# Modulation rows of a two-layer diffusion block: the eight row blocks of a weight tile in four column groups of TensorE

## The reference, cut to what matters

```python
# d = D_MODEL = 1024; w_mod: (DEPTH, d, 6 * d); b_mod: (DEPTH, 6 * d)
        mod_l = jax.nn.silu(c) @ w_mod[layer] + b_mod[layer]
        mod_c = jax.nn.silu(c_ctx) @ w_mod[layer] + b_mod[layer]
        sh1, sc1, g1, sh2, sc2, g2 = jnp.split(mod_l[:, None, :], 6, axis=-1)
        csh1, csc1, cg1, csh2, csc2, cg2 = jnp.split(mod_c, 6)
```

## Time and profile before

| | us |
|---|---|
| median of 3 runs | 3995.61 |
| lowest, highest | 3993.08, 3996.35 |
| the profiled execution's own time | 3988.36 |
| its span in the profile | 3986.6 |
| TensorE busy | 3170.7 (80%) |
| VectorE busy | 1925.9 (48%) |
| ScalarE, GpSimd busy | 739.1, 1444.5 |
| mean granted TensorE clock | 0.894 |

### The profile page before, as it was taken

How to read it: one execution, slowest core, us unless ns; L and a number is a source line. 1 busy time by engine, 2 the same in 40 slices (tenths; PEclk the granted TensorE clock), 3 DMA queues, 4 the chain that set the end, 5 groups by cost and what they waited for, 6 DMA issues and landing times. The chain is left out here.

```text
span 3986.6 us, 27787 instructions
## 1 busy us (share of the span) xinstructions
PE 3170.7 (80%) x8516; PEld 1539.3 (39%) x8516; DVE 1925.9 (48%) x4693; ACT 739.1 (19%) x1716; POOL 1444.5 (36%) x1540
## 2 busy tenths in 40 slices
PE   6978975688788888878749676688887597897888
PEld 2433433233333333333334234344333264543663
DVE  1014626766666667676440365766776314213100
ACT  0011321221212222221100311222212011122100
POOL 0000001777777777777600001777777200000000
PEclk8989787889999999989979698899898898998999
DMA  5114122999999999999932144999999642433333
GB/s 184 64 54 170 45 86 105 395 419 419 419 413 418 416 415 414 416 415 408 390 132 79 50 154 153 417 419 413 417 419 414 240 138 100 128 106 121 110 128 116
DMA packets 349203, 1028.16 MB, mean 258 GB/s; under 512 B 53620, under 2 KB 58228, under 8 KB 346996
## 3 DMA queue, kind: packets, MB, share of 16 engines
q0 software_dynamic: 221184, 805.40, 50.0%
q1 hardware_dynamic: 125808, 217.57, 15.8%
q10 hardware_dynamic: 2068, 3.47, 0.3%
HBM read 1025.19 MB, written 1.15 MB: 257 GB/s over the span
## 5 line engine op out<-in xcount | busy, mean ns | idle before, releaser
L1288 PE MATMUL l_peer_experts_acc<-l_peer_experts_ring,l_peer_experts_diag 128*128 128x512 f32 x3072 | 1490.9, 636 | 359.6 <-ACT l_peer_experts_diag L1328 293.3
L1221 POOL DMA_INDIRECT weight_slots<-in_peer_u,l_peer_experts_picks x768 | 722.2, 940 | 1394.6 <-DVE l_peer_experts_picks L1415 1144.3
L1463 DVE SCALAR_TENSOR_TENSOR weight_slots<-weight_slots,l_peer_experts_h 128x1024 f32<-128x1024 f32 x768 | 937.1, 1220 | 593.5 <-DMA weight_slots<-in_peer_u,l_peer_experts_picks 587.5
L1288 PEld LDWEIGHTS l_peer_experts_acc<-l_peer_experts_ring,l_peer_experts_diag 128*128 128x128 f32 x3072 | 606.0, 204 | 1195.0 <-issue 1001.9
L1226 POOL DMA_INDIRECT l_peer_experts_ring<-in_peer_v,l_peer_experts_picks x768 | 722.1, 940 | 295.9 <-issue 199.3
L1328 ACT ACTIVATE l_peer_experts_diag<-const_ident,l_peer_experts_wgt 128x128 f32<-128x128 f32 x768 | 229.5, 387 | 172.4 <-DVE l_peer_experts_wgt L1431 172.4
L1251 PE MATMUL l_peer_experts_queries<-h_t,l_query_weights 128*128 128x512 f32 (+3 forms) x576 | 180.5, 457 | 4.1 <-PEq L61 4.1
L1310 ACT ACTIVATE l_peer_experts_h<-h_tiles 128x1024 f32<-128x1024 f32 x48 | 49.3, 1027 | 614.7 <-DVE weight_slots L1463 614.7
L1251 PEld LDWEIGHTS l_peer_experts_queries<-h_t,l_query_weights 128*128 128x128 f32 x576 | 104.7, 197 | 76.2 <-issue 67.5
L1307 ACT ACTIVATE l_peer_experts_soft<-l_peer_experts_best,l_peer_experts_low 128x16 f32<-128x16 f32 x48 | 14.7, 307 | 580.8 <-DVE l_peer_experts_low L1394 580.8
L190 PE MATMUL b_mlp_acc<-weight_slots,b_up 128*128 128x512 f32 x256 | 111.6, 599 | 12.1 <-DVEq L282 12.1
(11 more groups left out here) (423 smaller groups left out, 3311.1 us busy)
## 6 DMA issues: line engine op xcount, KB each, us to landing
weight_slots<-in_w_mod SPq DMA_DIRECT2D x24, 2048.0 KB, 8.1
weight_slots<-in_w_in SPq DMA_DIRECT2D x20, 2048.0 KB, 7.9
l_query_weights<-query_weights SPq DMA_DIRECT2D x16, 1024.0 KB, 7.8
weight_slots<-in_w_mlp_up SPq DMA_DIRECT2D x8, 2048.0 KB, 8.0
weight_slots<-in_w_mlp_down SPq DMA_DIRECT2D x8, 2048.0 KB, 7.8
weight_slots<-in_peer_u,l_peer_experts_picks POOLq DMA_INDIRECT x768, 9.0
l_peer_experts_ring<-in_peer_v,l_peer_experts_picks POOLq DMA_INDIRECT x768, 9.0
weight_slots<-in_gla_w_in SPq DMA_DIRECT2D x6, 2048.0 KB, 9.0
```

The costliest lines, as they stand in the source:

```text
L1221: pool.indirect_dma_start(u_ring[:, k % RING, :], None, u, bass.IndirectOffsetOnAxis(ap=picks[:, b % 4, k:k + 1], axis=0)).then_inc(landed ...
L1288: ins = nc.tensor.matmul(acc[:, c * BANK:(c + 1) * BANK], diag[:, k, :], v_ring[:, k % RING, c * BANK:(c + 1) * BANK], start=(k == 0), sto ...
L1463: nc.vector.scalar_tensor_tensor(row, row, 1.0, hp[:, :], ALU.mult, ALU.mult, accum_out=dots[:, b % 2, k:k + 1]).then_inc(dotted, 1)
```

## The change

The eight products of a tile no longer go to the same two rows of the bank. `silu_c` becomes 128 x 8 x 32 with zeros behind the first two columns, and each product writes 32 rows of the bank by its own quarter of TensorE's columns: the n-th goes to column group n % 4 and takes row block 2 (n % 4) + n // 4, so each group adds up two row blocks. The bank then holds four partial sums of 32 rows each, of which two rows count. VectorE copies the bank to a buffer `mod_parts` (`vector_parts`), one more product with a constant 128 x 2 of zeros and ones, `add_up`, adds the four up into the bank's rows 0 and 1 (`tensor_sums`), and VectorE adds the bias from there (`vector`). `mod_bias` is gone: the bias is loaded into the row buffer itself, in which VectorE adds, so a bias load now waits for the store that reads the buffer. SyncE loads the next weights when the products are through (`multiplied`), not when the sum is.

```diff
@@ class Modulation
+    GROUPS = 4
+    PER = KC // GROUPS
...
-        self.bias_sb = st.sb("mod_bias", [2, 2, BANK])
         self.rows = st.sb("mod_rows", [2, 2, BANK])
-        self.used, self.taken = st.sem("mod_used"), st.sem("mod_taken")
+        self.parts = st.sb("mod_parts", [P, BANK])
+        self.multiplied, self.parted, self.used, self.taken = (st.sem(f"mod_{n}") for n in ("multiplied", "parted", "used", "taken"))
...
     def tensor(self, pe, u, units):
         for step in self.share(u, units):
-            i, k = divmod(step, KC)
+            i, n = divmod(step, KC)
             slot = (self.weights.n + i) % 2
-            if k == 0:
+            j, k = n % self.GROUPS, n % self.GROUPS * self.PER + n // self.GROUPS
+            if n == 0:
                 pe.wait_ge(self.weights.loaded[slot], self.weights.count(i, i // 2))
                 if i >= len(self.banks):
                     pe.wait_ge(self.taken, i - len(self.banks) + 1)
-            ins = self.nc.tensor.matmul(self.banks[i % len(self.banks)][0:2, :], self.silu_c[:, k, :], self.weights.slots[:, slot, k, :],
-                                        start=(k == 0), stop=(k == KC - 1))
-            if k == KC - 1:
-                ins.then_inc(self.used, 1)
+            ins = self.nc.tensor.matmul(self.bank(i)[32 * j:32 * j + 32, :], self.silu_c[:, k, :], self.weights.slots[:, slot, k, :],
+                                        start=(n < self.GROUPS), stop=(n >= KC - self.GROUPS), tile_position=(0, 32 * j))
+            if n == KC - 1:
+                ins.then_inc(self.multiplied, 1)
+
+    def tensor_sums(self, pe, u, units):
+        for step in self.share(u, units):
+            i, n = divmod(step, KC)
+            if n == KC - 1:
+                pe.wait_ge(self.parted, i + 1)
+                self.nc.tensor.matmul(self.bank(i)[0:2, :], self.add_up, self.parts[:, :], start=True, stop=True).then_inc(self.used, 1)
+
+    def vector_parts(self, dve, u, units):
+        for step in self.share(u, units):
+            i, n = divmod(step, KC)
+            if n == KC - 1:
+                dve.wait_ge(self.multiplied, i + 1)
+                if i:
+                    dve.wait_ge(self.used, i)
+                self.nc.vector.tensor_copy(self.parts[:, :], self.bank(i)).then_inc(self.parted, 1)
 
     def vector(self, dve, u, units):
...
             dve.wait_ge(self.used, i + 1)
             dve.wait_ge(self.bias_loaded[s], 16 * turn + 16)
-            if turn:
-                dve.wait_ge(self.stored[s], 16 * turn)
-            ins = self.nc.vector.tensor_tensor(self.rows[:, s, :], self.banks[i % len(self.banks)][0:2, :], self.bias_sb[:, s, :], ALU.add)
+            ins = self.nc.vector.tensor_tensor(self.rows[:, s, :], self.bank(i)[0:2, :], self.rows[:, s, :], ALU.add)
...
     def sync(self, sp):
         def bias(i):
             at = self.first + i * BANK
             if i < self.tiles:
-                sp.dma_start(self.bias_sb[:, i % 2, :], self.bias[at:at + BANK].partition_broadcast(2)).then_inc(self.bias_loaded[i % 2], 16)
+                if i >= 2:
+                    sp.wait_ge(self.stored[i % 2], 16 * (i // 2))
+                sp.dma_start(self.rows[:, i % 2, :], self.bias[at:at + BANK].partition_broadcast(2)).then_inc(self.bias_loaded[i % 2], 16)
...
         for i in range(self.tiles):
-            sp.wait_ge(self.used, i + 1)
+            sp.wait_ge(self.multiplied, i + 1)
             self.weights.load(sp, i + 2)
...
             sp.dma_start(self.mod_rows[:, at:at + BANK], self.rows[:, i % 2, :]).then_inc(self.stored[i % 2], 16)
-            bias(i + 2)
+            if i:
+                bias(i + 1)
@@ stage_conditions: nc.vector.memset(silu_c[:, :, :], 0.0), then
-                nc.scalar.activation(silu_c[:, :, :], cols[:, :, :], ACT.Silu)
+                act.wait_ge(cleared, 1)
+                nc.scalar.activation(silu_c[:, :, 0:2], cols[:, :, :], ACT.Silu)
@@ stage_first_modulation, TensorE
-                mod.tensor(pe, 0, 1)
+                for i in range(mod.tiles):
+                    mod.tensor(pe, i, mod.tiles)
+                    if i == 1:
+                        pe.wait_ge(add_up_loaded, 16)
+                    if i:
+                        mod.tensor_sums(pe, i - 1, mod.tiles)
+                mod.tensor_sums(pe, mod.tiles - 1, mod.tiles)
@@ stage_first_modulation, VectorE
-                mod.vector(dve, 0, 1)
+                for i in range(mod.tiles):
+                    mod.vector_parts(dve, i, mod.tiles)
+                    mod.vector(dve, i, mod.tiles)
@@ stage_mlstm, TensorE (the same line in stage_attention)
                     last.then_inc(out_done, 1)
+                    mod.tensor_sums(pe, u, len(units))
@@ stage_mlstm, VectorE
                     last.then_inc(w_ready, 1)
-                    mod.vector(dve, u, len(units))
+                    mod.vector_parts(dve, u, len(units))
...
                     dve.sem_inc(out_taken, 1)
+                    mod.vector(dve, u, len(units))
@@ stage_gla, TensorE
                     if u + 1 < n_units:
                         keys_values(u + 1)
+                    mod.tensor_sums(pe, u, n_units)
@@ stage_gla, VectorE
                     if u:
                         take_results(u - 1)
+                        mod.vector(dve, u - 1, n_units)
                     take_scores(u)
-                    mod.vector(dve, u, n_units)
+                    mod.vector_parts(dve, u, n_units)
                 take_results(n_units - 1)
+                mod.vector(dve, n_units - 1, n_units)
@@ constants
+    add_up = np.zeros((P, 2), np.float32)
+    for c in range(2):
+        add_up[c::32, c] = 1
```

More of the change, by code:

```diff
@@ L391, in __init__ @@
         assert planned == name, (planned, name)
-        self.nc, self.weights, self.silu_c, self.banks = nc, weights, silu_c, banks
+        self.nc, self.weights, self.banks = nc, weights, banks
+        self.silu_c, self.add_up = silu_c
         self.tiles = n // BANK
         self.bias, self.mod_rows, self.first = bias, mod_rows, first
-        self.bias_sb = st.sb("mod_bias", [2, 2, BANK])
         self.rows = st.sb("mod_rows", [2, 2, BANK])
-        self.used, self.taken = st.sem("mod_used"), st.sem("mod_taken")
+        self.parts = st.sb("mod_parts", [P, BANK])
+        self.multiplied, self.parted, self.used, self.taken = (st.sem(f"mod_{n}") for n in ("multiplied", "parted", "used", "taken"))
         self.bias_loaded = [st.sem(f"mod_bias_loaded{s}") for s in range(2)]
@@ L404, in share, with bank @@
         return range(u * self.tiles * KC // units, (u + 1) * self.tiles * KC // units)
+    def bank(self, i):
+        return self.banks[i % len(self.banks)]
     def tensor(self, pe, u, units):
         for step in self.share(u, units):
-            i, k = divmod(step, KC)
+            i, n = divmod(step, KC)
             slot = (self.weights.n + i) % 2
-            if k == 0:
+            j, k = n % self.GROUPS, n % self.GROUPS * self.PER + n // self.GROUPS
+            if n == 0:
                 pe.wait_ge(self.weights.loaded[slot], self.weights.count(i, i // 2))
@@ L414, in tensor @@
                     pe.wait_ge(self.taken, i - len(self.banks) + 1)
[L415 to L418 removed]
+            ins = self.nc.tensor.matmul(self.bank(i)[32 * j:32 * j + 32, :], self.silu_c[:, k, :], self.weights.slots[:, slot, k, :],
[16 more added lines that the diff above has]
+                self.nc.vector.tensor_copy(self.parts[:, :], self.bank(i)).then_inc(self.parted, 1)
     def vector(self, dve, u, units):
         for step in self.share(u, units):
[L422 to L423 removed]
+            i, n = divmod(step, KC)
+            if n != KC - 1:
                 continue
@@ L468, in stage_conditions, with _ @@
         cols = st.sb("cols", [P, KC, 2])
-        loaded = st.sem("loaded")
+        loaded, cleared = st.sem("loaded"), st.sem("cleared")
         with nc.Block() as block:
+            @block.vector
+            def _(dve):
+                nc.vector.memset(silu_c[:, :, :], 0.0).then_inc(cleared, 1)
             @block.sync
@@ L492, in _ @@
             def _(sp):
-                for dst, src in pairs:
-                    sp.dma_start(dst, src).then_inc(loaded, 16)
+                for i, (dst, src) in enumerate(pairs):
+                    sp.dma_start(dst, src).then_inc(loaded if i else add_up_loaded, 16)
                 mod.sync(sp)
-                sp.wait_ge(loaded, 16 * len(pairs))
+                sp.wait_ge(loaded, 16 * (len(pairs) - 1))
             @block.tensor
             def _(pe):
-                mod.tensor(pe, 0, 1)
+                for i in range(mod.tiles):
[5 more added lines that the diff above has]
+                mod.tensor_sums(pe, mod.tiles - 1, mod.tiles)
             @block.vector
             def _(dve):
-                mod.vector(dve, 0, 1)
+                for i in range(mod.tiles):
+                    mod.vector_parts(dve, i, mod.tiles)
+                    mod.vector(dve, i, mod.tiles)
     mod.done()
```

(19 more changed lines are left out.)

4 lines of the change are left out of this document (1 added, 3 removed).

## The result

The changed kernel takes 4044.15 us (median of 4 runs, 4040.54 to 4046.03) against 3995.98 for the kernel before: ratio 1.0119, 95% interval 1.0103 to 1.0135. It is 48 us slower; the forecast was 4002.6, its own range 3993 to 4010, and the range with the rivals went up to 4042.

The account below looks back on a forecast made before the run. Bounds read by stage: TensorE in `gla`, VectorE and ScalarE in odd `mlstm` units, row products in even ones. Terms -2.0 + 0.5 + 3.8 + 0.6 = +2.9, clock +4, gave +7 us: 4002.6 us, range 3993 to 4010.

Parts of the forecast that it names:

- Rival C: In all changed stages: column groups do not overlap, tile time stays 7.07 us, kernel 4040.6 us; chance 0.20.
- M: Time from a tile's first row product until VectorE may read it: 7.07 us before, forecast 4.07 us.
- rival B: In all changed stages: four column groups run together, tile time 1.92 us, kernel 3978.2 us; chance 0.33.
- the order rule: On TensorE: products start in program order, so paired records overlap only partly, 9 steps in place of 16, 4.07 us.
- gla: Stage `gla`: longer looped units, +7.0 us, offset by the last two at -3.4 us; together +0.6 us.
- The loop through the one bank: In `gla`: TensorE waits until VectorE takes the previous tile's row, making units 13.35 us against 12.4.
- mlstm: Stage `mlstm`: units sum to -0.7 us, but the last store comes later; +0.5 us, bounds -3 to +4.
- The late store at the end: End of `mlstm`: store issued 4.1 us later, at 390.5 against 386.4, landing at 393.9 against 393.4.
- the clock's term: TensorE at half clock after waits in five `gla` units: between 0 and 8.5 us, half taken, +4 us.
- rival D: Overlap by pairs, but half clock after every wait in `gla` and `mlstm`: +22 on 2.9, 4020.6 us; chance 0.07.
- mod0: Stage `mod0`: last load issued near 44 and not 46.56, landing near 52; -2.0 us.
- attn: Stage `attn`: one product per unit leaves nothing to overlap, and four sums come on top; +3.8 us.

Follow-up runs that it names:

- a_shift32: The changed kernel plus an unused 32-byte-per-partition SBUF buffer ahead of its constants, so gathered buffers start at multiples of 64 again: 3992.17 us, ratio 0.9997.
- a_order: `a_shift32` with both products of each column group issued as neighbours: 4255.94 us where the kernel before took 4257.09.
- a_mlstm_thrice: `a_shift32` with the eight products of each `mlstm` tile issued three times over: ratio to the kernel before 1.0005 (0.9976 to 1.0034).
- b_slots32_only_4: A repeat on the kernel before with `weight_slots` alone starting 32 past a multiple of 64, on a slow-gather chip; the five such repeats had ratios 0.9997 to 1.0020.

## Why the prediction was wrong

- **The step that failed: that the change acts in four stages only.** The first paragraph took "some 340 us of 3986.6 us" as all that could move (the four stretches that I had read add up to 370), and gave the new constant and the moved `silu_c` a zero ("Clearing `silu_c` and the small constant lie beside the first loads: 0"). I asked when the constant is loaded, not where it lies. Its 32 bytes moved the gathered buffers, and the expert stages lost 46.6 of the 52.2 us of span; in `a_shift32` these stages are back at 1335.2 and 684.9 us. Rival C's 4040.6 us is near the result by accident: its mechanism, no overlap, did not happen.
- **M, mis-sized.** Forecast 4.07 us, measured 1.92 at full clock: the lower bound, rival B. The step that failed here is the order rule, applied to the records of a product: `a_order` (1.94 to 1.95 us) shows that the groups do not wait for each other. So the rule that the prediction cites for it from the Trainium skill ("The mechanism": matmuls start and end strictly in program order) does not hold for the records of these f32 products. The span model in the same page, "TensorE: Matmul & The Clock Gate", section "Measured speedup vs the span model", agrees with the trace: four tiles cost about one (16 records in 1.92 us; four records in one group would take 4 x 0.43 = 1.72, an estimate from the pace in the earlier trace rows).
- **gla.** The loop through the one bank was right in each link: unit = 9.28 + M, here 12.9. But the tiles of the loop took 3.3 to 3.6 us, at half clock behind their waits; that this is near the forecast's 4.07 is luck. Rival B had given -17.4 with M = 1.92, the forecast +0.6; it was -9.6.
- **mlstm.** Forecast +0.5, measured +11.6. The late store at the end was right (398.26, and 10.4 us behind the last load, so that the load no longer ends the stage). What failed is the clock's term: half of 8.5 us, put on `gla`. Faster products opened waits of 3.15 to 3.30 us in `mlstm` ahead of the products that VectorE waits for, and the eight groups of output products became 1.2 to 2.2 us longer, 12.5 together, the greater part of it on the path: with the clock kept up in `a_mlstm_thrice` the stage is still 3.7 us longer than before. The prediction had the 4.7 us wait of an odd unit in its rival B, and gave it no price; its rival D did price a fall in all eight units, at 1.7 us each, with a chance of 0.07.
- **mod0.** Forecast -2.0, measured -2.8; with this stage's code as before the same point was reached 0.7 us earlier to 1.2 us later in the table, so the size is not sharper than that.
- **attn.** Forecast +3.8, measured +5.8, and this tells nothing: with the code of before, this stretch took 153.9 to 181.8 us in the table, by the clock it was given (in `a_shift32`, 187.2 us, the window 396 to 580 has 0.68).
- **The sum outside the expert stages** was +5.6 against a forecast of +7, by errors that cancel: -9.6 and +11.6 where I had +0.6 and +0.5. As measured without the address loss (`a_shift32`), the change is worth nothing: 0.9997 (0.9982 to 1.0013).

## What to carry to other kernels

Look at where a change puts every later buffer, not only at the one that it adds: compare the start addresses before and after, and keep what a fast gather writes at a multiple of 64 bytes. When the time moves and the changed stages do not explain it, set the two traces side by side over the whole program before forming a theory. A change that makes TensorE's work shorter than what another engine does in the same unit opens a wait; price the products behind this wait at half clock too, for here they were slower in 20 of 24 units of `mlstm`. Filling the wait with useless products kept the clock up, but won only 0.6 us of the stage; a second bank that removes the wait for the row won 10 us of `gla`.

## What the runs showed of the hardware that was not expected

- Gathers of 4 KB rows into SBUF ran at 416 to 417 GB/s with destinations at multiples of 64 bytes and at 406 with either destination 32 past one. Weight loads of 2 MB, in pieces of 2 KB, did not suffer: their groups landed in 7.7 to 9.0 us (medians) with `weight_slots` at a multiple of 64 and in 7.7 to 8.4 us with it 32 past one. The Trainium skill, "DMA: Bandwidth & Descriptors", section "How a descriptor splits into AXI transactions", says that the first transaction of a descriptor that does not start at a multiple of 256 bytes begins at the boundary below it, and that the unused bytes cost time too. Applied to destinations in SBUF, the runs differ from that: `weight_slots` at 192 past a multiple of 256 (before) and at a multiple of 256 (`a_shift32`) gave 416 and 417 GB/s, the ring at 64 past one 416. Slow were only starts 32 past a multiple of 64.
- On some chips the same kernel before took 4238 to 4266 us and not 3985 to 3996, and variants of it had their gathers at 358 to 371 GB/s; why is not shown. There the 32 bytes of one buffer cost at most 0.4% (the highest interval, that of `b_slots32_only_4`, is 1.0000 to 1.0040), against 1.04 to 1.06% where the gathers were fast.
- Four column groups of TensorE ran at once in f32, in both orders of the products that were tried: 16 records in 1.92 to 1.95 us, against 7.03 in one group.
- Useless products in a wait kept the output products of `mlstm` at 2.50 us in eight of eight units, where without them 20 of 24 took 3.64 to 4.67 us. In the same stage waits of 3.28 us were followed by half clock in some units and by full clock in others.
